# Search rounds ahead of the attention loop, zero rows on ScalarE's queue, and ScalarE copies for the second tile of each head

## The reference, cut to what matters

```
score[t,s] = sum_h w[t,h] * relu(q_idx[t,h] . k_idx[s])     # 4 index heads, causal
keep the topk = min(256, 512 // 4) = 128 best keys of each row t
o = softmax(q k^T over the kept keys) v                      # 6 sparse heads
```

## Time and profile before

| | us |
|---|---|
| median of 3 runs | 2157.55 |
| the profiled execution | 2156.96 |
| its span, first to last instruction | 2155.2 |
| PE busy (11384 instructions) | 1975.8 (92%) |
| DVE busy (2338) | 1204.0 (56%) |
| ACT busy (1402) | 850.7 (39%) |
| POOL busy (447) | 524.3 (24%) |

### The profile page before, as it was taken

How to read it: one execution, slowest core, us unless ns; L and a number is a source line. 1 busy time by engine, 2 the same in 40 slices (tenths; PEclk the granted TensorE clock), 3 DMA queues, 4 the chain that set the end, 5 groups by cost and what they waited for, 6 DMA issues and landing times. The chain is left out here.

```text
span 2155.2 us, 30251 instructions
## 1 busy us (share of the span) xinstructions
PE 1975.8 (92%) x11384; PEld 1718.4 (80%) x11384; DVE 1204.0 (56%) x2338; ACT 850.7 (39%) x1402; POOL 524.3 (24%) x447
## 2 busy tenths in 40 slices
PE   6998898999999999889899999998998989799994
PEld 6898787888888889878788888878986878677773
DVE  3557875444543454787544453379922243488885
ACT  4354454222211344455421221133234452277772
POOL 2665421000000256533100000025543444200001
PEclk9999898999999999999999999999999999799997
DMA  4112322313221111232232322125657732689995
GB/s 163 60 60 68 85 84 115 126 63 117 102 73 59 53 68 43 79 94 67 108 131 83 117 82 93 59 100 108 108 138 233 206 127 108 230 326 410 409 410 199
DMA packets 73534, 288.80 MB, mean 134 GB/s; under 512 B 18241, under 2 KB 23105, under 8 KB 48961
## 3 DMA queue, kind: packets, MB, share of 16 engines
q1 hardware_dynamic: 64768, 255.67, 35.1%
q10 hardware_dynamic: 6048, 22.02, 2.6%
q0 software_dynamic: 2592, 9.44, 1.2%
HBM read 244.14 MB, written 37.19 MB: 131 GB/s over the span
## 5 line engine op out<-in xcount | busy, mean ns | idle before, releaser
L1295 PE MATMUL fill_ps<-w_hi,h_hi 128*128 128x256 f32 (+1 forms) x704 | 210.2, 299 | 7.9 <-PEq L3161 5.1
L1295 PE MATMUL fill_ps<-w_hi,h_lo 128*128 128x256 f32 (+1 forms) x704 | 205.3, 292 | 0.0
L1295 PE MATMUL fill_ps<-w_lo,h_hi 128*128 128x256 f32 (+1 forms) x704 | 205.0, 291 | 0.0
L322 POOL TENSOR_SCALAR norm_ss<-norm_ss 128x1 f32<-128x1 f32 x24 | 4.8, 201 | 796.3 <-ACT ffn_raw_d L316 739.0
L845 POOL TENSOR_TENSOR w_lo<-w_raw,w_hi 128x512 fp32r<-128x512 f32 x120 | 162.2, 1376 | 143.3 <-ACT w_hi L913 143.1
L516 DVE TENSOR_TENSOR ffn_silu<-ffn_silu,ffn_up 128x512 f32<-128x512 f32 x44 | 30.2, 687 | 286.6 <-ACT ffn_silu L474 286.6
L1792 POOL TENSOR_TENSOR w_lo<-w_raw,w_hi 128x512 fp32r<-128x512 f32 x96 | 144.7, 1535 | 137.6 <-ACT w_hi L1876 137.6
L474 ACT ACTIVATE ffn_silu<-ffn_up 128x512 f32<-128x512 f32 x44 | 26.3, 598 | 337.1 <-PE ffn_up L575 337.1
L528 DVE TENSOR_TENSOR x<-ffn_down,x 128x512 f32<-128x512 f32 x176 | 119.1, 689 | 71.2 <-PE ffn_down L590 70.4
L575 PE MATMUL ffn_up<-h_hi,w_hi 128*128 128x512 f32 x384 | 152.1, 396 | 3.5 <-PEq L792 3.5
L1295 PEld LDWEIGHTS fill_ps<-w_hi,h_hi 128*128 128x128 f32 x704 | 142.0, 202 | 13.1 <-issue 10.6
(11 more groups left out here) (454 smaller groups left out, 5352.3 us busy)
## 6 DMA issues: line engine op xcount, KB each, us to landing
moe_raw_gu<-in_w_e_gu SPq DMA_DIRECT2D x46, 1024.0 KB, 11.2
w_raw<-in_w_mix SPq DMA_DIRECT2D x28, 1024.0 KB, 5.0
w_raw<-in_w_two SPq DMA_DIRECT2D x23, 1024.0 KB, 5.2
moe_raw_d<-in_w_e_down SPq DMA_DIRECT2D x23, 1024.0 KB, 7.9
w_raw<-in_w_gate SPq DMA_DIRECT2D x22, 1024.0 KB, 5.6
w_raw<-in_w_up SPq DMA_DIRECT2D x22, 1024.0 KB, 6.7
ffn_raw_d<-in_w_down SPq DMA_DIRECT2D x22, 1024.0 KB, 4.9
moe_in<-in_zero SPq DMA_DIRECT2D x23, 512.0 KB, 8.0
```

The lines of the kernel that those rows point to most:

```text
L322: self.core.nc.gpsimd.tensor_scalar(s_t, s_t, 1.0 / D, NORM_EPS, ALU.mult, ALU.add).then_inc(self.rooted, 1)
L1295: last = nc.tensor.matmul(b[:, 0:cols], aw[:, k, t * P:(t + 1) * P], ww[:, k, 0:cols], start=k == 0 and n == 0, stop=k == KD - 1 and n == 2)
```

## The change

Five things are changed, the first three in the mixer of both layers, the last in the second mixer.

1. The index scores move forward: the turns come in the middle of chunk 2, the scores after its last two tiles and after the first tile of chunk 3. ACT's copies and relus, and DVE's weighing, follow that order. Eight rounds of the search, not three, run ahead of the loop; `sum_squares(2)` now stands behind the sixth of them (before: ahead of the first), and `normalise(2, 0)` behind the seventh (before: behind the first). In the loop 16 half rounds are left of 26.
2. The dense parts of chunks 8 to 10 are dealt out to other steps; units 12 and 13 are turned one step later (19 and 21), and weight chunk 9 is split one step earlier (18).
3. ACT instead of DVE copies the turned probabilities of tile 1 (256 columns) of each of the 20 heads.
4. In the second mixer SP starts its first stack rows when `outputs_within` is done (new semaphore `within_summed`), not when both state-space products are.
5. The 23 zero rows leave SP's queue. ACT issues them, one in each of the steps 9 to 31 of the relative attention.

The diff, cut to its core:

```diff
-TOP_EARLY = 3
+TOP_EARLY = 8
...
-    DENSE.setdefault(_n // 3 if _n < 36 else 12 + (_n - 36) * 11 // 12, []).append(_x)
-UNIT_AT = {4: 4, 5: 5, 8: 6, 9: 7, 12: 8, 13: 9, 16: 10, 17: 11, 18: 12, 20: 13, 26: 14, 28: 15, 44: 16, 45: 17, 51: 18, 56: 19}
+    DENSE.setdefault(_n // 3 if _n < 36 else 12 + (_n - 36) * 3 // 4 if _n < 48 else 22 + (_n - 48) * 11 // 12 if _n < 60 else _n - 27, []).append(_x)
+UNIT_AT = {4: 4, 5: 5, 8: 6, 9: 7, 12: 8, 13: 9, 16: 10, 17: 11, 19: 12, 21: 13, 26: 14, 28: 15, 44: 16, 45: 17, 51: 18, 56: 19}
...
-SPLIT_AT = {6: 0, 7: 4, 8: 8, 9: 19, 10: 25, 11: 36, 12: 45, 13: 60, 14: 72, MIX_CHUNKS: 83}
+SPLIT_AT = {6: 0, 7: 4, 8: 8, 9: 18, 10: 25, 11: 36, 12: 45, 13: 60, 14: 72, MIX_CHUNKS: 83}
...
-SEARCH_AT = {_n: _j for _j, _n in enumerate(_m for _m in range(44) if _m % TB < 2 or _m in (22, 26, 30, 34))}
+SEARCH_AT = {_n: _j for _j, _n in enumerate((0, 1, 5, 8, 17, 20, 21, 24, 25, 28, 29, 32, 33, 36, 40, 41))}
...
+                        if c == 2 and t == 2:
+                            for m, dst in enumerate((iq_t[0], iq_t[1], ik_t)):
+                                act.wait_ge(idx_turned, m + 1)
+                                nc.scalar.copy(dst, bank("idx", m)[:]).then_inc(idx_out, 1)
                         evict(c, t)
+                        if c == 2 and t >= 2:
+                            relu_of(t - 1)
...
-                for m, dst in enumerate((iq_t[0], iq_t[1], ik_t)):
-                    act.wait_ge(idx_turned, m + 1)
-                    nc.scalar.copy(dst, bank("idx", m)[:]).then_inc(idx_out, 1)
                 for t in range(TB):
                     evict(3, t)
-                    if t < TB - 1:
-                        relu_of(t + 1)
+                    if t == 0:
+                        relu_of(TB - 1)
...
-                    if 2 <= n < STEPS + 2 and (n - 2) % TB >= 2:
+                    if 2 <= n < STEPS + 2 and (n - 2) % TB >= 1:
...
+                weigh(1)
+                weigh(2)
                 sum_squares(1)
-                normalise(1, 0)
...
-                for i in BLK:
-                    weigh(i)
+                weigh(TB - 1)
+                normalise(1, 0)
                 dve.wait_ge(weighed, 3 * IDX)
...
-                sum_squares(2)
                 for r in range(TOP_EARLY):
                     find(r)
                     take(r)
-                    if r == 0:
+                    if r == TOP_EARLY - 3:
+                        sum_squares(2)
+                    if r == TOP_EARLY - 2:
                         normalise(2, 0)
...
-                    if 2 <= n < STEPS + 2 and (n - 2) % TB < 2:
+                    if 2 <= n < STEPS + 2 and (n - 2) % TB < 1:
...
-                    if n == TB * (TOPK // 8 - TOP_EARLY):
+                    if n == 52:
...
+                        if c == 2 and t == 2:
+                            pe.wait_ge(idx_ready, 1)
+                            for m in range(3):
+                                turn_idx(m)
...
+                        if c == 2 and t >= 2:
+                            if t == 2:
+                                pe.wait_ge(idx_out, 3)
+                            score_idx(t - 1)
...
-                pe.wait_ge(idx_ready, 1)
-                for m in range(3):
-                    turn_idx(m)
...
-                    if t < TB - 1:
-                        if t == 0:
-                            pe.wait_ge(idx_out, 3)
-                        score_idx(t + 1)
+                    if t == 0:
+                        score_idx(TB - 1)
...
+ZERO_AT = 9
...
-
-                def zero_rows(first, last):
-                    for b in range(first, min(last, BLOCKS)):
-                        sp.dma_start(core.moe_in[b * P:(b + 1) * P, :], w["zero"].partition_broadcast(P)).then_inc(emptied, 16)
...
@@ -1750,7 +1755,7 @@
                         sp.wait_ge(maxed, TB * (j - 1))
                     sp.dma_start(bias[j % 2], w["rel"][j]).then_inc(bias_in[j % 2], 16)
...
-                        sp.wait_ge(y_summed, 1)
+                        sp.wait_ge(within_summed, 1)
                     if j >= 2:
...
                         sp.dma_start(glu_in[:], core.y_save.rearrange("(f p) n -> p f n", p=P)).then_inc(y_back, 16)
                     for c in REL_LOAD_AT.get(j, ()):
                         load(c)
...
@@ -2017,6 +2021,9 @@
                         copy_pt(n - 2)
...
+                    if 0 <= n - ZERO_AT < BLOCKS:
+                        b = n - ZERO_AT
+                        act.dma_start(core.moe_in[b * P:(b + 1) * P, :], w["zero"].partition_broadcast(P)).then_inc(emptied, 16)
...
-                        nc.tensor.matmul(y_of(g), within[:, g, :], u_c[:, g, :], start=g // 2 % 8 == 0, stop=False)
+                        last = nc.tensor.matmul(y_of(g), within[:, g, :], u_c[:, g, :], start=g // 2 % 8 == 0, stop=False)
+                    last.then_inc(within_summed, 1)
```

More of the change, by code:

```diff
@@ L744, in mixer @@
         stacked = [sem("stacked0"), sem("stacked1")]
-        order = [("dense", n) for n in range(3 * TB)] + [("idx", n) for n in range(3)]
-        order += [("dense", n) for n in range(3 * TB, 5 * TB - 1)] + [("unit", 0), ("unit", 1), ("dense", 5 * TB - 1), ("unit", 2), ("unit", 3)]
+        order = [("dense", n) for n in range(3 * TB - 2)] + [("idx", n) for n in range(3)]
+        order += [("dense", n) for n in range(3 * TB - 2, 5 * TB - 1)] + [("unit", 0), ("unit", 1), ("dense", 5 * TB - 1), ("unit", 2), ("unit", 3)]
         for n in range(LAST + 1):
@@ L771, in dve_copies @@
         def dve_copies(n):
-            return sum(1 for m in range(n) if m % TB < 2)
+            return sum(1 for m in range(n) if m % TB < 1)
         def group(p):
@@ L1366, in turn_probs @@
                         copies = dve_copies(n - 1)
-                        if (n - 2) % TB < 2:
+                        if (n - 2) % TB < 1:
                             pe.wait_ge(pt_dve, copies)
@@ L1377, in value @@
                     copies = dve_copies(n + 1)
-                    if i < 2:
+                    if i < 1:
                         pe.wait_ge(pt_dve, copies)
@@ L1633, in second_mixer @@
         stacked = [sem("stacked0"), sem("stacked1")]
+        within_summed = sem("within_summed")
         norm = RouteNorm(core, "m2", [gate1a[:, n * D:(n + 1) * D] for n in range(2)], rel_bias[:, 0:D], banks[2:6],
@@ L1766, in _ @@
                         load(c)
-                    zero_rows(3 * j, 3 * j + 3)
                 sp.wait_ge(emptied, 16 * BLOCKS)
```

## The result

The changed kernel takes 2175.26 us, the median of five runs (2169.94 to 2180.62), beside 2158.45 for the kernel before (2155.32 to 2159.57). The ratio on record is 1.0084, 95% interval 1.0064 to 1.0104: some 17 us slower by the medians, 18 by the ratio. The forecast was 2160 with a range to 2171.

A forecast was written before the change was run, and what follows sets the result against it. The prediction took PE as the bound: fronts +9.3 and +10.6, loops -3.4, second mixer -12.9, +3.6 in all on 2157.55, giving 2161.1, placed at 2160; own range 2154 to 2166, 8-in-10 range 2147 to 2171.

The forecast's parts named there:

- I take 79: Front of the first layer: search rounds start at 79 us, chosen between 77.5 and a slow end of 81.0.
- +9.3: First layer's front: sum_squares(2) starts at 98.3, not 89.03, so the first score comes 9.3 us later.
- +10.6: Second layer's front: first score 10.6 us later, as the new front lacks a slack of 1.3.
- the stack's wait in the loop: PE's 2.0 us loop wait for a stack's DMA: priced at +2.2 a layer, expected to measure 3 to 5.
- the wait of 4.6: PE's loop wait for a bank DVE frees: moving the take and tile copy gives -1.9, leaving 3 or less.
- The second layer's extra 1.3: Second layer's front: the old front absorbed a slack of 1.3 us that the new one cannot, adding 1.3.
- The loop, -3.4: Attention loops of both layers: shorter PE waits and a lighter DVE give -1.7 us a layer, -3.4 together.
- rival E: Loop: DVE's normalise, not the take, decides PE's 4.6 us wait; +2.9 a layer, 2166; chance 0.18 shared with the lower-clock case.
- The second mixer, -12.9: Second mixer: PE's waits for stack rows go (-2.3 and -8.2), clock recovers (-2.4): -12.9 us, bounds -15 to -3.
- B: Loop: half of PE's 16.3 us idle a layer hangs on DVE, so lighter DVE gives 8.1 a layer; 2147, chance 0.28.
- C: Ahead of each loop: PE's long stand lowers its clock, +3.5 us a layer; 2167, chance 0.18 including the 4.6 wait staying.
- D: Second mixer: zero rows only change queue and still delay later heads' stacks, +10 us; 2170, chance 0.16.

The follow-up runs named there:

- the first edit: Changed kernel with POOL's split of chunk 4 moved ahead of its root norm_root(1): 2168.71 us, ratio 1.0050 to the kernel before.
- the second edit: Changed kernel with the gate sums behind the first tile of chunk 3 and its index score, not ahead: 2176.28 us, ratio 1.0069 to the kernel before.
- the second mixer alone: Kernel before with only the change's second mixer (early stack rows, zero rows on ACT): 2144.11 us, ratio 0.9929; run again 2142.51, ratio 0.9928.
- seven rounds ahead with the old tables: Changed kernel, seven early rounds, sum behind the third, chunk 4 split early, gate sums late, DENSE, UNIT_AT, SPLIT_AT as before: 2148.53 us, ratio 0.9952.

## Why the prediction was wrong, point by point

**The step that failed is "I take 79": the start of the search rounds.** It was 84.37, beyond even the slow end of 81.0. The mechanism was the one forecast: the sum late, POOL's tail of 14 unchanged, PE standing at the unit turns. The size of its term was off: +9.3 was worked out, +14.5 measured in the first layer, and +10.6 against 14.7 in the second.

Along the two traces the whole is this. The changed kernel is behind by 14.5 at the first score, 13.2 at the last turn of the first layer, 28.0 at the second layer's first score, 26.0 at its last turn, 30.0 at the state-space products, 16.7 at the last row maximum of the second mixer and 18.2 at the end. So the fronts cost 29.3 (forecast 19.9), the loops -3.3 (-3.4), the second mixer -13.3 (-12.9). The 9.4 of the fronts takes the forecast of 2160 to some 2169, the upper end of the range. What carries the time past it is 5.5 in stretches that the forecast put at nothing, as their code does not differ: 4.0 ahead of the state-space products, and 1.5 behind the second mixer:

```profile
1571.77 1.45 PE L2433 MATMUL bank<-ssm_all 128*128 128x64 f32 x12
```

```profile
1601.77 1.45 PE L2440 MATMUL bank<-ssm_all 128*128 128x64 f32 x12
```

(before, then after).

The 5.4 us between 79 and 84.4 are made up of four parts. By 2.0 the figure of 79 lay below the forecast's own slow end of 81.0, which is added up from rows. The largest part is the weighing: from the start of the last score to its end it took 3.3 longer than there. It was taken as it stood in the trace of before, where POOL had nothing to do beside it (its split of chunk 4 was over at 75.3, the weighing began at 83.2). The new order brings the two together, and the first edit above, which parts them, takes 2.8 us off the weighing. A further 1.3 is on PE. The last score started late, as the tile ahead of it, from 69.98, took 4.5 and not 3.07 us: it ran at the lower clock (0.83 in 70 to 80 above) behind the gate sums, and at full clock (1.00 in 70 to 80) in the second edit, which moves these away.

```profile
74.51 2.93 PE L1338 MATMUL s_ps<-mix_out 64*128 64x512 f32 x8
```

The forecast had 73.2. The other way, some -1.2: `normalise(1, 0)` took 1.21, not the 2.29 of the earlier trace rows, where it ran beside POOL's split. The lower end of 77.5 rested on waits and lower clock going away, and pulled the middle down. The rows that would have told of the weighing were there, in the kernel before:

```profile
72.81 3.32 DVE L1134 SCALAR_TENSOR_TENSOR topk_work<-prob_t,topk_iw,topk_work 128x256 f32<-128x256 f32 x3
...
83.82 2.46 DVE L1134 SCALAR_TENSOR_TENSOR topk_work<-prob_t,topk_iw,topk_work 128x512 f32<-128x512 f32 x3
```

The weighing of the smallest tile took 3.32 us beside POOL's split of chunk 4 (69.05 to 75.26), the largest one without it 2.46.

**The signs.** PE's stand (15.1), the stack's wait in the loop (3.1) and the stack waits of the second mixer (none) came as named. The first score (117.98, not 111 to 115), the sum (103.62, not 97 to 100) and the wait of 4.6 (3.9, not 3 or less) did not.

**The second layer's extra 1.3** is not confirmed: its front lost 14.7, the first layer's 14.5.

**The loop, -3.4.** On the traces of the changed kernel: -1.3 for the first layer (first score to last turn: 14.54 to 13.21) and -1.9 for the second. That this comes out beside -3.4 is luck. The loop of the changed kernel's first layer is 225.4 us; the trace of before has 226.8, but three other traces of the same untouched mixers (the second mixer alone, twice, and without the move of the zero rows) have 224.4 to 225.6, so no gain of the loop is shown there. The single waits were off: the stack's grew by 1.1, not 2.2, and the wait of 4.6 fell by 0.7, not by 1.9. As in rival E, the `take` does not decide it. But the trace puts its end down to more than DVE's normalise. DVE and POOL after, then DVE before:

```profile
243.49 1.23 DVE L1076 TENSOR_TENSOR rope_a<-dsa_qk,const 128x128 f32<-128x128 f32 x1
```

```profile
238.40 6.18 POOL L845 TENSOR_TENSOR w_lo<-w_raw,w_hi 128x512 fp32r<-128x512 f32 x4
```

```profile
230.86 0.29 DVE L1073 TENSOR_TENSOR rope_a<-dsa_qk,const 128x128 f32<-128x128 f32 x1
```

With the `take` gone, this operation of 0.29 comes soon enough to stand beside POOL's split and ends with it (244.72 and 244.58); the `store` that frees PE's bank follows. Before, its neighbour ended with POOL's split (230.83 and 230.68). The time that the `take` gave up went to POOL, as in the front.

**The second mixer, -12.9:** right in kind and in size. By the ratio it alone gives -15.5, of which the traces have some 3 us ahead of it, in mixers that were not touched; its own steps are 13.3 to 13.4 shorter in the changed kernel and in the second trace of the second mixer alone, and 10.8 in the first. The parts fit as well: -3.2 with the semaphore alone (forecast -2.3), and 10.1 more with the zero rows moved (forecast 8.2 and 2.4). The forecast's bound of -15, put together from 11.6 and the clock's 2.4, adds up to -14.0.

**Rivals.** B, that the lighter DVE pays in the loop, fell: seven rounds ahead with the old tables are some 5 us slower than the kernel with three, where B has a gain of 16. C, the lower clock behind the stand, cost nothing: it fell on the last tile of chunk 4, in POOL's tail (0.66 from 112 to 116), and the loop began at full clock:

```profile
118.00:128.00 10.00, 9.52 (x77) 9.31 (x78) 5.25 (x22) 5.87 (x11) 7.97 (x9) 1.00 0.01 4
```

D, the zero rows still in the way, fell: in the changed kernel no head waited for its stack. The Trainium skill (DMA: Bandwidth & Descriptors, "Issuing engines are not separate DMA queues") would give the move of the zero rows to another issuer only the time of their issue, 2.1 us for three. By the ratios it gave some 10. The trace agrees that both issuers share the 16 engines (51% of their time for SP's DMAs and 17% for ACT's, from 1603 to 1693). But the move changed the time too: ACT issues its first zero row at 1652.69, 43 us after the first stack rows, while SP had issued nine within 39. Whether the stack rows were late because they stood in SP's line behind the zero rows, or because these flowed beside them, is not shown: no run left them on SP and issued them later.

**Left open:** the 4.0 us between the end of the second layer and the state-space products in the changed kernel, where no code differs. The kernel with late gate sums has 3.5 there, the others between 0 and 2.2, and the two traces of one and the same kernel (the second mixer alone) 1.6 and 0.0. In the changed kernel two waits of PE there are longer, one for DVE by 2.2 us and one for POOL's low part of a weight (3.6 for 2.0); why they are is open. The 1.5 behind the second mixer is as open: the two traces of that one kernel have 6.1 and 1.9 there.

## What to carry to other kernels

Work moved ahead on an idle engine is only free up to the point where something short stands behind it in that engine's order: here a reduction of 1.2 us, the head of a 14 us chain through another engine, paid for six rounds of search. Put the short head of a long chain first and fill behind it. And when a reordering is priced with durations from the old trace, look at which other engine ran beside them there, and which will run beside them in the new order.

## What the runs showed of the hardware

DVE's operations with two SBUF inputs and POOL's subtraction of weights hold each other up, and by whole operations. The normalise of 1024 columns took 1.21 with POOL idle and 2.31 beside its split; the three masks 0.68 alone, and 3.79 beside the split, to its end; the last weighing 3.1 and 6.3. Its first operation, with one such input and a scalar for each partition, was held too (0.48 and 1.18). POOL's four operations took 5.01 with the weighing out of the way and 6.10 beside it. The search's own operations were not touched: a round was 3.22 beside POOL's split in the kernel before, and 3.23 beside an idle POOL. The Trainium skill (SBUF — State Buffer, "SBUF: two separate sides") has a pair of ports that DVE and GpSimd share as an exclusive lock for a whole instruction, taken by a DVE operation with two SBUF inputs against a GpSimd one that reads SBUF. The trace agrees, in that the masks of 0.2 us each waited out an operation of POOL of 1.5.
